# Per-layer gate product of a hybrid decoder block: from tile-by-tile rows to seven products on pairs of tiles

## The reference, cut to what matters

```python
x = x + mix @ w_out
h = rmsnorm(x, g_ffn)
gu = h @ w_gate_up
x = x + (silu(gu[..., :D_FF]) * gu[..., D_FF:]) @ w_down
gate = sigmoid(rmsnorm(x, g_ple_gate) @ w_ple_gate)     # the product that is changed
e = rmsnorm(p @ w_ple_up, g_ple_post)
x = x + gate * e
return rmsnorm(x, g_final)
```

## Time and profile before

| | us |
|---|---|
| median of three runs | 1017.89 |
| lowest, highest | 1017.25, 1017.89 |
| the profiled execution's own time | 1018.0 |
| its span, first to last instruction | 1015.5 |
| TensorE matmul busy, share of the span | 1004.8, 99% |
| VectorE (DVE) | 714.1, 70% |
| ScalarE (ACT) | 426.1, 42% |
| GpSimd (POOL) | 383.7, 38% |

### The profile page before, as it was taken

How to read it: one execution, slowest core, us unless ns; L and a number is a source line. 1 busy time by engine, 2 the same in 40 slices (tenths; PEclk the granted TensorE clock), 3 DMA queues, 4 the chain that set the end, 5 groups by cost and what they waited for, 6 DMA issues and landing times.

```text
span 1015.5 us, 12378 instructions
## 1 busy us (share of the span) xinstructions
PE 1004.8 (99%) x4615; PEld 835.3 (82%) x4615; DVE 714.1 (70%) x945; ACT 426.1 (42%) x639; POOL 383.7 (38%) x285
## 2 busy tenths in 40 slices
PE   8999999999999999999999999999999999999997
PEld 7888888888888888888888888888888888888886
DVE  5899999956699575575575575575678785865454
ACT  6725438414363433433433433433444554554333
POOL 3356797710146444444444444441000000024282
PEclk9999999999999999999999999999999999999998
DMA  7421202652224234234234234215995988614112
GB/s 251 136 83 42 82 2 103 209 172 76 104 63 135 74 108 130 74 109 128 76 109 128 75 108 130 74 68 180 370 392 195 323 270 279 193 42 166 63 63 84
DMA packets 103501, 138.77 MB, mean 137 GB/s; under 512 B 6114, under 2 KB 60914, under 8 KB 103442
## 3 DMA queue, kind: packets, MB, share of 16 engines
q1 hardware_dynamic: 103442, 137.99, 40.3%
HBM read 105.20 MB, written 32.77 MB: 136 GB/s over the span
## 4 chain that ended last, share of the span: by engine, by line
PE 98%; DVE 1%; ACT 0%; issue 0%; POOL 0%; POOLq 0%; DVEq 0%; ACTq 0%
PE ps L1272 32%; PE ps L1274 31%; PE ps L1273 31%; PE ps L1318 2%; PE ps L1325 0%; PE ps L1331 0%; PE ps L1417 0%; PE ps L1407 0%; DVE act_lo L1654 0%; PE ps L1397 0%; ACT junk L841 0%; DVE scr L1681 0%; DVE ring_lo L1654 0%; ACT scr L1265 0%; DVE gtmp L1907 0%
## 5 line engine op out<-in xcount | busy, mean ns | idle before, releaser
L595 POOL TENSOR_SCALAR ss<-ss 128x1 f32<-128x1 f32 x39 | 14.5, 371 | 333.6 <-ACT junk L841 328.1
L1743 DVE SCALAR_TENSOR_TENSOR ps<-resid,convw,ps 128x512 f32<-128x512 f32 x190 | 127.4, 745 | 0.0
L1272 PE MATMUL ps<-ring_hi,ring_lo 128*128 128x512 f32 x308 | 120.1, 390 | 0.1
L1274 PE MATMUL ps<-ring_hi 128*128 128x512 f32 x308 | 119.9, 389 | 0.0
L1273 PE MATMUL ps<-ring_lo,ring_hi 128*128 128x512 f32 x308 | 119.8, 389 | 0.0
L1272 PE MATMUL ps<-act_hi,bs_lo 128*128 128x512 f32 x240 | 93.6, 390 | 0.0
L1274 PE MATMUL ps<-act_hi,bs_hi 128*128 128x512 f32 x240 | 93.4, 389 | 0.0
L1273 PE MATMUL ps<-act_lo,bs_hi 128*128 128x512 f32 x240 | 93.4, 389 | 0.0
L1654 DVE TENSOR_TENSOR ring_lo<-raw,ring_hi 128x512 fp32r<-128x512 f32 x89 | 57.9, 687 | 32.0 <-ACT ring_hi L826 32.0
L826 ACT ACTIVATE ring_hi<-raw 128x512 fp32r<-128x512 f32 x89 | 51.9, 626 | 67.0 <-PE ps L1274 67.0
L601 POOL TENSOR_TENSOR wc_lo<-raw_b,wc_hi 128x1024 fp32r<-128x1024 f32 x22 | 58.8, 2675 | 47.9 <-ACT wc_hi L826 46.8
(11 more groups left out here) (206 smaller groups left out, 2628.5 us busy)
## 6 DMA issues: line engine op xcount, KB each, us to landing
raw<-in_w_gate_up SPq DMA_DIRECT2D x44, 512.0 KB, 5.3
raw<-in_scratch SPq DMA_DIRECT2D x52, 256.0 KB, 4.0
raw<-in_w_down SPq DMA_DIRECT2D x52, 256.0 KB, 4.8
in_scratch<-in_s SPq DMA_DIRECT2D x44, 256.0 KB, 2.8
in_scratch<-gtmp SPq DMA_DIRECT2D x33, 256.0 KB, 2.3
keep<-in_w_down SPq DMA_DIRECT2D x32, 256.0 KB, 5.0
keep<-in_scratch SPq DMA_DIRECT2D x25, 256.0 KB, 4.4
resid<-in_x SPq DMA_DIRECT2D x8, 512.0 KB, 7.8
```

What stands on the lines that cost most here:

```text
L595: pool.tensor_scalar(ss[:, n:n + 1], ss[:, n:n + 1], 1.0 / D, EPS, ALU.mult, ALU.add)\
L1272: pe.matmul(dst, w_lo_, m_hi, start=start, stop=False, skip_group_check=onto)
L1274: return pe.matmul(dst, w_hi_, m_hi, start=False, stop=stop, skip_group_check=onto)
L1743: dve.scalar_tensor_tensor(out=conv_c if k == last_odd else acc, in0=u_all[:, c, k + h * BANK:k + (h + 1) * BANK], scalar=convw[:, c * 32 ...
```

## The change

The product of the gate is computed on pairs of tiles (256 positions) in the seven-product form: the 1024 channels are cut in two halves, the 1024 output columns in two halves, the pair in its two tiles. Each of the seven products has four k blocks. Product numbers are those of the code: 1, 2, 6, 5, 7, 3, 4.

- **Norm weights.** g_ple_gate is no longer multiplied onto x: it is loaded at the start with the other small vectors (one more small DMA, one transpose with 24 rows in place of 16) and multiplied as a column onto the rows of w_ple_gate (pg_scale, ScalarE). The norm of x is then a plain scaling by 1/rms, on ScalarE (gate_norm), where it was a VectorE instruction.
- **Weight forms.** For each of four k: SP loads two row blocks (k and k + 4), ScalarE scales both (steps 28, 35, 42 and 58), GpSimd forms four differences of 128x512 (gate_weights), ScalarE and VectorE split the seven forms (pg_high, pg_low). That is 28 copies and 28 lows of 128x512 in place of 8 and 8 of 128x1024, spread over steps 29 to 65.
- **Data forms.** Per pair, ScalarE copies a21 and VectorE forms four sums (sums, last_sum); the seven operand forms are split (even, odd, sum highs and lows).
- **Behind the products.** ScalarE copies three partial results, VectorE adds onto them (gate_11, gate_22, gate_12), ScalarE applies four sigmoids of half width per pair. VectorE's final multiply is now in place, in x.
- **Order.** The first transposes stand in step 72 and behind the last step, where they stood in steps 71 and 73. The last pair's columns come in the order shown at the end of the diff. The last store is issued by ScalarE.

The diff, cut:

```diff
...
-        PG_STEP = {29: 0, 32: 1, 35: 2, 38: 3, 42: 4, 47: 5, 60: 6, 63: 7}
-        PG_LOAD = {24: 0, 25: 1, 28: 2, 33: 3, 37: 4, 41: 5, 55: 6, 58: 7}
+        PG_ORDER = tuple((i, k) for k in range(4) for i in (1, 2, 3, 5, 6, 7)) + tuple((4, k) for k in range(4))
+        PG_SCALE = {28: 0, 35: 1, 42: 2, 58: 3}
+        PG_STEP = {29: (0,), 30: (1,), 31: (2,), 32: (3,), 33: (4, 5), 36: (6,), 37: (7,), 38: (8,), 39: (9,),
+                   40: (10, 11), 43: (12, 13), 44: (14,), 45: (15,), 46: (16,), 51: (17,), 59: (18,), 60: (19,),
+                   61: (20,), 62: (21, 22), 63: (23, 24), 64: (25, 26), 65: (27,)}
+        PG_LOAD = {28: 0, 29: 1, 38: 2, 39: 3, 45: 4, 46: 5, 61: 6, 62: 7}
...
+            if i in (1, 2, 3):
+                return scr[:, min(i - 1, 1), (BANK if i == 3 else 0):(2 * BANK if i == 3 else BANK)]
+            if i in (6, 5):
+                return row_part(bs_raw, 2 * (6 - i), k)
+            if i == 7:
+                return keep[:, 4 * k + 2, :]
+            return scr[:, 2, k * BANK:(k + 1) * BANK] if k < 2 else pw_raw[:, :] if k == 2 else gain[:, 0:BANK]
...
             for n, src in enumerate((conv_b, ln_g, ln_b, pool_scale)):
                 sp.dma_start(scr[KC * n:KC * (n + 1), 2, C:C + P], src[0].rearrange("(c p) -> c p", p=P))\
                   .then_inc(const_in, DMA)
+            sp.dma_start(scr[4 * KC:4 * KC + KD, 2, C:C + P], g_ple_gate[0].rearrange("(c p) -> c p", p=P))\
+              .then_inc(const_in, DMA)
             load_stripe(0, 1, raw_in)
             load_stripe(1, 1, raw_in)
             load_x(6, xres[:, 6, :])
...
                 if n in PG_LOAD:
-                    k = PG_LOAD[n]
-                    if k >= 3:
-                        sp.wait_ge(pg_lo, k - 2)
-                    sp.dma_start(scr[:, k % 3, :], w_pg_v[:, k, :]).then_inc(pg_in, DMA)
-                if n == 5 * PAIRS + 2:
-                    sp.wait_ge(et_ok, 3 * PAIRS)
-                    load_gain(g_ple_gate[0])
+                    k, r = divmod(PG_LOAD[n], 2)
+                    if k and r == 0:
+                        sp.wait_ge(pg_lo, 6 * (k - 1) + 3)
+                        sp.wait_ge(pg_t34, 2 * k)
...
+            def gate_weights(k):
+                pool.wait_ge(pg_scaled, 2 * (k + 1))
+                if k == 0:
+                    pool.wait_ge(d_mm, len(ORDER))
+                if k == 3:
+                    pool.wait_ge(et_ok, 3 * PAIRS)
+                pool.tensor_tensor(pg_raw_form(5, k), scr[:, 0, C1], scr[:, 0, C0], ALU.subtract).then_inc(pg_t12, 1)
+                pool.tensor_tensor(pg_raw_form(7, k), scr[:, 1, C1], scr[:, 0, C1], ALU.subtract).then_inc(pg_t34, 1)
+                pool.wait_ge(pg_t12, 2 * k + 1)
+                pool.tensor_tensor(pg_raw_form(6, k), scr[:, 1, C1], pg_raw_form(5, k), ALU.subtract).then_inc(pg_t12, 1)
+                pool.wait_ge(pg_t12, 2 * k + 2)
+                pool.tensor_tensor(pg_raw_form(4, k), scr[:, 1, C0], pg_raw_form(6, k), ALU.subtract).then_inc(pg_t34, 1)
+
...
+            def pg_scale(k):
+                act.wait_ge(pg_in, 2 * DMA * (k + 1))
+                for r in range(2):
+                    copy(scr[:, r, :], scr[:, r, :], pg_scaled, scale=gcol[:, k + 4 * r:k + 4 * r + 1])
...
+            def gate_norm(t):
+                n = 2 * TT + t
+                act.wait_ge(rs_ok, n + 1)
+                if t >= 2:
+                    act.wait_ge(turned, 2 * n - 2)
+                else:
+                    act.wait_ge(et_ok, 3 * PAIRS + 2 * (t + 1))
+                copy(xg_place(t), x_tile(t, 2).rearrange("p (a n) -> p a n", a=2), xn_ok, scale=rs[:, n:n + 1])
...
+            for m in range(1, PAIRS_G - 1):
+                sigmoid_21(m - 1, C0)
+                odd_high(m)
+                act.wait_ge(e_sq, 2 * m + 1)
+                if m == 1:
+                    square_odd(6)
+                gate_p1(m)
+                if m == 1:
+                    square_odd(7)
+                square_out(2 * m - 2)
+                gate_norm(2 * m + 2)
+                square_out(2 * m - 1)
+                gate_u2(m)
+                gate_norm(2 * m + 3)
+                sigmoid(0, c11_ok, QUADS + m + 1)
+                even_high(m + 1)
+                gate_p5(m)
+                a21_copy(m + 1)
+                square_e(2 * m + 1, 3 * TT + 2 * m)
+                sigmoid(3, c22_ok, QUADS + m + 1)
+                for i in (6, 5, 7, 3):
+                    sum_high(m + 1, i)
+                sigmoid(1, c12_ok, QUADS + m + 1)
+                square_e(2 * m + 2, 3 * TT + 2 * m)
+            m, t = PAIRS_G - 1, TT - 1
...
+            sigmoid_21(m, CA)
+            sigmoid_21(m, CB)
+            act.wait_ge(res_ok, t + 2)
+            square_half(t - 1, C1, 5 * TT, 3 * TT + 9)
+            act.wait_ge(res_ok, t + 3)
+            square_half(t, CA, 5 * TT + 1, 3 * TT + 10)
+            act.wait_ge(res_ok, t + 4)
+            square_half(t, CB, 5 * TT + 2, 3 * TT + 11)
             act.wait_ge(rs_ok, 4 * TT)
-            act.wait_ge(xg_ok, 3)
-            act.activation(scr[:, (TT - 1) % 2, BANK:D], scr[:, (TT - 1) % 2, BANK:D], ACT.Copy,
-                           scale=rs[:, 4 * TT - 1:4 * TT]).then_inc(fin_act_ok, 1)
+            act.wait_ge(xg_ok, 1)
+            last = raw[:, 2, C0]
+            act.activation(last, last, ACT.Copy, scale=rs[:, 4 * TT - 1:4 * TT]).then_inc(fin_act_ok, 1)
+            act.wait_ge(fin_act_ok, 1)
+            act.dma_start(out_v[EVEN_ODD[t]][:, C1], last).then_inc(out_stored[1], DMA)
...
-            pe.wait_ge(const_in, 5 * DMA)
+            pe.wait_ge(const_in, 6 * DMA)
...
+            def gate_part(m, i):
+                bank = gx(m) if i in (1, 6, 7, 4) else gz(m)
...
+                    last = product(ps[:, bank, :], x_form(i, 0)[:, k, :], x_form(i, 1)[:, k, :],
+                                   pg_hi_form(i, k), pg_lo_form(i, k), i in (1, 2, 5) and k == 0, k == 3, i in (6, 7, 4, 3))
                 last.then_inc(pg_mm, 1)
+
+            turn(1, 2)
+            pe.wait_ge(pg_lo, len(PG_ORDER))
+            for m in range(PAIRS_G):
+                gate_part(m, 1)
+                gate_part(m, 2)
+                gate_part(m, 6)
+                if m + 1 < PAIRS_G:
+                    turn(2 * m + 2, 2)
+                gate_part(m, 5)
+                if m + 1 < PAIRS_G:
+                    turn(2 * m + 3, 2)
+                gate_part(m, 7)
+                gate_part(m, 3)
+                gate_part(m, 4)
...
+                for k in PG_STEP.get(n - 1, ()):
+                    pg_low(k)
...
+            for m in range(1, PAIRS_G - 1):
+                gated(2 * m - 2, 4 * m - 1, 2 * m - 1)
+                gated(2 * m - 1, 4 * m, 2 * m)
+                gate_11(m)
+                odd_low(m)
+                final(2 * m - 2)
+                final(2 * m - 1)
+                even_low(m + 1)
+                sums(m + 1)
+                gate_22(m)
+                last_sum(m + 1)
+                sum_low(m + 1, 6)
+                sum_low(m + 1, 5)
+                gate_12(m)
+                sum_low(m + 1, 7)
+                sum_low(m + 1, 3)
+            m, t = PAIRS_G - 1, TT - 1
+            gated(t - 3, 4 * m - 1, t - 2)
+            gated(t - 2, 4 * m, t - 1)
+            gate_11(m)
+            odd_low(m)
+            final(t - 3)
+            final(t - 2)
+            gated(t - 1, 4 * m + 1, t, C0)
+            gate_22(m)
+            gated(t, 4 * m + 2, t + 1, C1)
+            gate_12(m)
+            dve.wait_ge(res_ok, t + 1)
+            dve.tensor_tensor(raw[:, 2, C0], x_tile(t, 3)[:, C1], raw_b[:, 1, C1], ALU.mult).then_inc(xg_ok, 1)
+            gated(t - 1, 4 * m + 3, t + 2, C1)
+            gated(t, 4 * m + 4, t + 3, CA)
+            gated(t, 4 * m + 5, t + 4, CB)
+            final(t - 1)
+            final(t, C0)
...
```

More of the change, by code:

```diff
@@ L164, in hybrid_block @@
         e_stored = [sem(f"e_stored{j}") for j in range(2)]
-        e_in = [sem(f"e_in{t}") for t in range(TT)]
+        e_in = [sem(f"e_in{j}") for j in range(3)]
         gfin_in = sem("gfin_in")
@@ L265, in hybrid_block @@
         pg_in = sem("pg_in")
+        pg_t12 = sem("pg_t12")
+        pg_t34 = sem("pg_t34")
+        pg_scaled = sem("pg_scaled")
         const_mm = sem("const_mm")
@@ new lines, in hybrid_block, with g_done, gx, gz @@
+        PAIRS_G = TT // 2
+        G_ORDER = (1, 2, 6, 5, 7, 3, 4)
+        FA, FS = 3 * HT, HT
+        def g_done(m, i):
+            return 7 * m + G_ORDER.index(i) + 1
+        def gx(m):
+            return 6 if m % 2 == 0 else 0
+        def gz(m):
+            return gx(m) + 1
+        def odd_bank(m):
+            return 4 if m else 0
+        def row_part(w, first, k):
+            return w[:, first + k // 2, (k % 2) * BANK:(k % 2 + 1) * BANK]
+        def pg_hi_form(i, k):
+            if i in (1, 2):
+                return row_part(ws_hi, 2 * (i - 1), k)
+            if i in (6, 5):
+                return row_part(bs_hi, 2 * (6 - i), k)
```

(68 more changed lines are left out.)

478 lines of the change are left out of this document (297 added, 181 removed).

## The result

| | us |
|---|---|
| before, median of five runs beside it | 1017.89 (1017.23 to 1018.05) |
| after, median of five runs | 1022.65 (1022.01 to 1023.63) |
| ratio, 95% interval | 1.0052 (1.0041 to 1.0063) |
| predicted | 1014.6, range 1008.0 to 1020.5 |
| profiled execution after: own time, span | 1023.36, 1021.6 |

The change makes the kernel slower by 0.5%. The prediction had the wrong sign, and the result lies outside its range. Up to 704 us both traces are the same within 0.1 us, so the span's growth of 6.1 us (from 1015.5) is made behind that.

The account below looks back on a forecast made before the run. TensorE's work plus its waits was taken as the bound. 1018.0 - 11.3 (matmuls) + 6.4 (down projection delays) + 0.7 (gate stage) + 0.8 (tail) = 1014.6 us, range 1008.0 to 1020.5.

Parts of the forecast that it names:

- TensorE's work: Gate stage: 384 matmuls (87.8 us) become 336 (76.4 us), so TensorE work falls by 11.4, taken as 11.3.
- The walk in order: Gate stage, first loop: scaled tile 4 ready at 944.5, wanted at 944.0, so 0.5, plus 0.2 for handovers: 0.7 us.
- GpSimd holds ring_lo: Down projection: four GpSimd subtractions after each scaling exclude VectorE's ring_lo for the whole 5.2 us, alternating 1.3 and 0.55.
- Step 28: Down projection, first pile-up: rows early, ring_lo of step 30 ends at 786.0, TensorE wanted it at 785.35: 0.7 us lost.
- step 58: Down projection, last pile-up: no delay inherited, 0.5 us lost.
- the landing, "I take 4.0": Down projection: new weight row loads land in 4.0 us, ends 3.4 and 5.9; ScalarE wants them after about 3.8.
- The prediction's own slope: Down projection: each microsecond of later landing costs 3 us, since delay is inherited.
- the weight rows come late, slower: Rival, ScalarE's wait at step 42: landings of 5.9 cost the down projection 12.1, giving 1020.3 us; chance 0.23.
- The clock: Rival: stalls at 36/37 and 43/44 each bring one step at the lower clock, 5.4 us, 1020.0 to 1020.2; chance 0.07.
- The tail, 0.8: After the last matmul: last store issued at 4.7 instead of 4.3, +0.4, and a larger store in flight, +0.4; bounds 0 to 1.5.
- The sum: Whole kernel: 1018.0 - 11.3 + 6.4 + 0.7 + 0.8 = 1014.6 us.
- VectorE did not bound the gate stage: Rival, gate stage: GpSimd's multiplies bring VectorE to 22.0 us a pair against TensorE's 20.85; 3.5 more, 1018.1; chance 0.12.

Follow-up runs that it names:

- the zero-filling run: Changed kernel with GpSimd's four differences of the weight rows replaced by zero fills, row loads left whole: 1011.72 us, ratio 0.9942.
- the run with small rows: Changed kernel with weight row loads cut to 8 of 1024 columns for the last three of four k, differences kept: 1014.87 us, ratio 0.9973.

## Why the prediction was wrong, by its own steps

**TensorE's work.** The removal of 11.3 us was right: 83.65 for the gate stage is 81.65 of work (76.4 and six turns of 0.87, as before) and 2.0 of waits and handovers. Predicted were 0.7. The excess is the 1.08 at 956.28, where the square of tile 6 stands ahead of gate_p1(1) on ScalarE, and 0.24 at 959.51. The walk in order had put the first lateness at the turn of tile 4, of 0.5; it missed this one. Off by 1.3.

**GpSimd holds ring_lo.** Right: 1.3 for GpSimd, then 0.5 for VectorE, 1.77 for a VectorE instruction where the row of before had 1.75. The rule of the Trainium skill, page SBUF — State Buffer, section Who interferes with whom, holds here for ring_lo; its other half, that a GpSimd instruction which only writes does not contend, is borne out by the zero-filling run (690 ns). Step 28, with its rows early, cost 0.15 as a wait (0.4 with the start), where 0.7 was walked; step 58, where 0.5 was walked, had waits of 0.74 and 0.39.

**The failed step: the landing, "I take 4.0".** The step says that SP's loads "come with no x rows beside them and no pile of held-back issues". The issue was not at fault: by the walk the second row of k = 1 goes out at 793.2 (landed 797.2, less 4.0), and it went out at 792.42. But the landings were 6.1 and 7.0 us for k = 1, and 4.5 and 7.0 for k = 2. The stretches in question, after and, below it, before:

```profile
790.00:799.00 9.00, 9.00 (x41) 7.46 (x40) 5.87 (x10) 3.19 (x6) 0.00 (x0) 1.00 0.93 335
816.00:825.00 9.00, 9.00 (x41) 7.46 (x40) 4.59 (x8) 2.32 (x4) 0.00 (x0) 1.00 1.00 364
```

```profile
790.00:799.00 9.00, 9.00 (x42) 7.44 (x41) 5.86 (x9) 4.41 (x7) 0.00 (x0) 1.00 0.97 340
816.00:825.00 9.00, 9.00 (x42) 7.44 (x41) 7.41 (x12) 4.11 (x8) 0.00 (x0) 1.00 0.82 268
```

The DMA engines are busy 93 and 100% of that time, mostly with the down projection's own operands (the two rows of k = 1 are 1.0 of the 3.0 MB moved in the first stretch). The first could have been read beforehand: before, it shows 0.97, and the mean of 0.75 over 107 us hid it. So could the landing itself. The quiet row of 3.4 us at 783.9 was the shortest of the eight in the kernel before; the next one, issued at 791.42 with no x row beside it and 0.8 us after the moment of the first new load, took 5.6, the others 5.2 to 8.2:

```profile
L561 SPq DMA_DIRECT2D scr<-in_w_ple_gate x1: 328/328/328, 791.4 to 791.4; - x1
...
DMA to landing us min/median/max: 5.6/5.6/5.6
```

The second stretch showed 0.82 before and 1.00 after. There SP, which stands 21.8 us in eleven waits for ring_lo between 785 and 825, issues ten loads in 4.7 us (813.39 to 818.08): 3.1 MB, where 364 GB/s move 1.7 in that time. That is a pile such as the step took to be absent. It needs no wait of TensorE ahead of it: in the run without differences there was none, and the second row of k = 2 took 7.8.

What that was worth: the down projection lost 13.7, of which 4.2 are the clock (below), so waits and starts took 9.5 where 6.4 was walked. The prediction's own slope, 3 us per microsecond of landing, would have given 6.4 + 3 x 3.0 = 15.4 for landings of 7.0. That this lies near 13.7 is luck, for the slope has no clock in it, and against 9.5 it is too steep. With landings of 3.4 to 4.4 in the run with small rows the time was 1014.87 against a forecast of 1014.6; here too errors cancel (the gate stage and the tail cost 2.2 more than forecast, the down projection 0.8 less, the time outside the span 0.7 less, and the down projection began 0.7 earlier). So the mechanism of the rival "the weight rows come late, slower" is what happened, and its condition of 5.8 us was met. It had no clock in its price of 12.1.

**The clock.** It had a chance of 0.07 as a case by itself, on the ground that no walked stall was longer than 2.0. The stalls were 3.05 and 4.02, and both brought the clock down, for 1.5 and 2.7 us of matmul time: 4.2 against the 5.4 worked out. This is the second failed step, and the larger one in microseconds: the sum has the clock at nothing, and this loss and the late rows were set as separate cases, although the longer stall brings the other with it. Without the 4.2 the median would have been about 1018.5 (an estimate: 1022.65 less 4.2), inside the range and little above before.

**The tail, 0.8.** It was 1.7. In the kernel after, from the squares' last sum on:

```profile
1015.19 1.29 DVE L2381 SCALAR_TENSOR_TENSOR resid<-resid,rs,raw_b 128x1024 f32<-128x1024 f32 x1 [0.45 <-POOL rs L937]
1015.26 1.39 POOL L939 TENSOR_SCALAR ss<-ss 128x1 f32<-128x1 f32 x1
1016.73 0.19 POOL L943 TENSOR_TENSOR ss<-ss 128x1 f32<-128x1 f32 x1
1017.00 0.56 POOL L945 TENSOR_TENSOR rs<-ss,neg_half 128x1 f32<-128x1 f32 x1
```

GpSimd's instruction on one column, 0.56 us for its twin at 1013.89, takes 1.39 beside VectorE's multiply. The prediction applied this exclusion to the down projection and not to the tail, where it put the power at 3.9 after the last matmul. The last store's issue is at 1018.37, 6.0 after the last matmul's end (some 1012.3), not 4.7.

**The sum.** From the span before, 1015.5: -11.3 + 13.7 + 2.0 + 1.7 = 1021.6, the span after. Outside the span the profiled execution after has 1.8 us and the one before 2.5, so its time grew by 5.4 and not by 6.1; the forecast held these 2.5 for fixed. Against the forecast's terms the down projection is 7.3 too small, the gate stage 1.3, the tail 0.9. Of the rivals, VectorE did not bound the gate stage (73.71 us busy in 97, above).
